# Both heads at once in the RWKV-7 core: products on four quarter tiles, joined evictions, and three reordered stage edges

## The reference

```python
def step(state, inp):
    r_t, w_t, k_t, v_t, a_t, b_t = inp
    sa = jnp.einsum('bhvk,bhk->bhv', state, a_t)
    state = state * w_t[:, :, None, :] + sa[..., None] * b_t[:, :, None, :] + v_t[..., None] * k_t[:, :, None, :]
    y = jnp.einsum('bhvk,bhk->bhv', state, r_t)
    return state, y
...
y = wkv7_scan(rf, decay, kd, vf, -kk, kk * a, reverse=(dirn == 1))
```

```python
q = rope_slice(rms_norm(q, q_gain), cos, sin, 0)
k = rope_slice(rms_norm(k, k_gain), cos, sin, 0)
```

## Time and profile before

| what | us |
|---|---|
| median of three runs | 2857.4 |
| lowest and highest run | 2849.94, 2857.96 |
| the profiled execution | 2856.87 |
| its span, first to last instruction | 2855.0 |
| PE busy | 2743.1 (96%) |
| DVE busy | 1465.4 (51%) |
| ACT busy | 1268.8 (44%) |
| POOL busy | 1127.8 (40%) |
| matmuls of the core's products, L779, busy | 291.5 |

### The profile page before, as it was taken

The page is one execution under the profiler, slowest core; times in us unless marked ns, Lnnn a source line. Parts: engine busy times, 40 slices in busy tenths (PEclk is TensorE's granted clock), DMA queues, the critical chain, the costliest instruction groups (busy, mean ns, idle before and its releaser), DMA issues.

```text
span 2855.0 us, 54997 instructions
## 1 busy us (share of the span) xinstructions
PE 2743.1 (96%) x23332; PEld 2187.8 (77%) x23332; DVE 1465.4 (51%) x2561; ACT 1268.8 (44%) x2296; POOL 1127.8 (40%) x634
## 2 busy tenths in 40 slices
PE   7899999979999999999999999999999999999999
PEld 5568888857778888877888876577777777788887
DVE  7865886057757777753888303612222224344410
ACT  5664443233556555644444225534444454422221
POOL 4124444534543332314444454034333443544443
PEclk9999999999999999999999999999999999999999
DMA  5102332322300000012233232023221332333232
GB/s 164 49 31 90 95 96 90 95 96 82 102 23 6 7 8 7 6 46 71 92 96 94 88 99 66 23 89 98 75 75 52 96 96 74 96 96 96 88 95 77
DMA packets 63460, 208.88 MB, mean 73 GB/s; under 512 B 11248, under 2 KB 11504, under 8 KB 62832
## 3 DMA queue, kind: packets, MB, share of 16 engines
q1 hardware_dynamic: 60704, 193.10, 21.9%
q0 software_dynamic: 1936, 10.91, 1.1%
q10 hardware_dynamic: 576, 1.35, 0.1%
HBM read 199.95 MB, written 4.19 MB: 72 GB/s over the span
## 4 chain that ended last, share of the span: by engine, by line
PE 86%; DVE 9%; ACT 2%; issue 2%; POOL 1%; DMA 0%; SPq 0%; DVEq 0%; ACTq 0%
PE banks L1658 21%; PE banks L1660 21%; PE banks L1659 21%; PE banks L779 9%; PE banks L1800 1%; DVE low L539 1%; PE banks L830 1%; DVE arena L2641 1%; PE banks L772 1%; PE banks L856 1%; PE banks L1776 1%; PE banks L1695 1%; PE banks L861 1%; PE banks L872 1%; PE banks L1848 1%
## 5 line engine op out<-in xcount | busy, mean ns | idle before, releaser
L312 POOL TENSOR_TENSOR low<-arena,high 128x1024 fp32r<-128x1024 f32 (+1 forms) x376 | 876.7, 2332 | 1328.8 <-ACT high L303 1328.7
L1658 PE MATMUL banks<-high,high 128*128 128x512 f32 (+1 forms) x2752 | 1093.4, 397 | 40.9 <-POOL low L312 24.1
L1660 PE MATMUL banks<-high,low 128*128 128x512 f32 (+1 forms) x2752 | 1082.3, 393 | 0.0
L1659 PE MATMUL banks<-low,high 128*128 128x512 f32 (+1 forms) x2752 | 1082.3, 393 | 0.0
L303 ACT ACTIVATE high<-arena 128x1024 fp32r<-128x1024 f32 (+1 forms) x376 | 381.9, 1016 | 800.9 <-PE banks L1660 799.5
L1658 PEld LDWEIGHTS banks<-high,high 128*128 128x128 f32 x2752 | 519.9, 189 | 171.6 <-POOL low L312 18.0
L1660 PEld LDWEIGHTS banks<-high,low 128*128 128x128 f32 x2752 | 519.9, 189 | 120.7
L1659 PEld LDWEIGHTS banks<-low,high 128*128 128x128 f32 x2752 | 520.2, 189 | 118.6 <-issue 1.9
L779 PE MATMUL banks<-arena 64*64 64x64 f32 x7680 | 291.5, 222 | 9.7 <-DVE arena L1544 3.4
L779 PEld LDWEIGHTS banks<-arena 64*64 64x64 f32 x7680 | 251.2, 135 | 58.1 <-issue 23.8
L2538 DVE TENSOR_TENSOR arena<-banks,arena 128x512 f32<-128x512 f32 x48 | 33.1, 691 | 425.1 <-PE banks L1660 423.9
(11 more groups left out here) (292 smaller groups left out, 2915.9 us busy)
## 6 DMA issues: line engine op xcount, KB each, us to landing
arena<-weights SPq DMA_DIRECT2D x302, 512.0 KB, 3.5
arena<-weights SPq DMA_DIRECT2D x48, 448.0 KB, 3.2
arena<-weights SPq DMA_DIRECT2D x28, 256.0 KB, 2.6
arena<-tables POOLq DMA_DIRECT2D x5, 448.0 KB, 3.6
arena<-x_t SPq DMA_DIRECT2D x4, 512.0 KB, 5.8
x_spill<-arena POOLq DMA_DIRECT2D x1, 2048.0 KB, 9.3
arena<-small_weights POOLq DMA_DIRECT2D x16, 128.0 KB, 2.6
arena<-x_spill POOLq DMA_DIRECT2D x1, 2048.0 KB, 9.3
```

The lines of the kernel that those rows point to most:

```text
L312: pool.tensor_tensor(lo[:, 0:n], ring[w % RING][:, 0:n], hi[:, 0:n].bitcast(F32), ALU.subtract).then_inc(w_low, 1)
L1658: pe.matmul(dst, hi[:, c], x[0], start=kt == 0, stop=False)
L1659: pe.matmul(dst, hi[:, c], x[1], start=False, stop=False)
L1660: mm = pe.matmul(dst, lo[:, c], x[0], start=False, stop=kt == kts_of[t] - 1)
```

## The change

Products. `both_heads` issues the products of both heads in one loop. Head 0 writes output half p from input half p as before, head 1 writes output half 1-p, each to the bank of its head, so the two fill all four quarters. S1, S2, U2, U5, U6, Q1 and Q2 go through it; S3, U3, U4 and T stay with `product`. Where head 1's result is the right factor of a later product, it lies in the other half of the partitions; for U2 POOL therefore writes U1 of head 1 a second time in swapped halves (UX, two instructions of 64x128 between U1_0 and U1_1).

Evictions. ACT copies S1, S2, Q1 and Q2 of both heads in one instruction of 128x512 over two banks, where it had two of 128x256; DVE adds U2, U5 and U6 in one of 128x256, where it had two of 128x128. Each waits for the second head's product, and the next product of either head waits for it. S1 waits for D_1 instead of D_0 for its first head.

Iteration 0. The table load goes ahead of S1's eviction, the copy of a1's hidden rows behind T's; POOL's k_sum goes ahead of the three low parts; the split of rw_g1's first tile goes to iteration 4.

Edges. (a) `sines(last)` goes behind `value(1)`, into the attention at its fourth step. (b) a_q's weights are split ahead of the biases, and each bias product follows one a_k tile. (c) Three score products go ahead of the last head sum, the fourth stays behind.

```diff
@@ def pe_rwkv
+        def both_heads(into, col, lhs, rhs):
+            last = [None, None]
+            for q in range(2):
+                for p in range(2):
+                    for h in range(2):
+                        last[h] = pe.matmul(into[h][hf(p ^ h), col + C * q:col + C * q + C], lhs(hf(p), h, q), rhs(hf(p), h, q),
+                                            start=True, stop=True)
+            return last
...
-        def square(i, h, s):
+        def square(i, s):
             if s == 1:
-                d2.wait(pe, i, f"D_{h}")
-                m, mt = (lambda r, q: R.D[r, h, q, :]), half_of(R.NM, h, 0)
+                d2.wait(pe, i, "D_1")
+                m, mt = (lambda r, h, q: R.D[r, h, q, :]), halves_of(R.NM, 0)
             else:
-                a2.wait(pe, i, f"S{s - 1}_{h}")
...
+                a2.wait(pe, i, "S1")
+                m, mt = halves_of(R.P2, 0), halves_of(R.P2, 1)
+            both_heads(PJ, 0, mt, m)
+            mm = both_heads(PJ, P, m, mt)
+            for h in range(2):
+                p2.inc(mm[h], f"S{s}_{h}")
...
+        def first_grow(i):
+            d2.wait(pe, i, "M_1")
+            g2.wait(pe, i, "U1_1")
+            mm = both_heads(PI, 0, halves_of(R.P2, 1), lambda r, h, q: R.UX[r, q, :] if h else R.U[i % 2][r, 0, q, :])
+            for h in range(2):
+                p2.inc(mm[h], f"U2_{h}")
...
+        def late_grow(i, m):
+            a2.wait(pe, i, f"Q{m}")
+            mm = both_heads(PI, 0, halves_of(R.P2, 1), halves_of(R.P2, 0))
...
+            d2.wait(pe, i, "U4_1" if m == 1 else "U5")
+            both_heads(PJ, 0, halves_of(R.NM, m), u)
+            mm = both_heads(PJ, P, u, lambda r, h, q: eye[r, :])
...
@@ the loop over iterations on PE
-                for s in (2, 3):
-                    for h in range(2):
-                        square(i, h, s)
-                        grow(i, h, s)
+                square(i, 2)
+                first_grow(i)
+                for h in range(2):
+                    last_square(i, h)
+                    grow(i, h, 3)
...
-                for h in range(2):
-                    merge(i, h, 1)
-                for h in range(2):
-                    grow(i, h, 5)
+                merge(i, 1)
+                late_grow(i, 1)
...
@@ def act_rwkv
+            def both(name, dst):
+                p2.wait(act, i, f"{name}_1")
+                a2.inc(act.activation(dst.rearrange("p h k b -> p h (k b)"), both_j[:, :, 0:256], ACT.Copy), name)
...
+                if i == 0:
+                    act.preload_act_table_set("natural_log_exp_and_others")
...
-                for h in range(2):
-                    ev("S1", h, flat(R.P2[:, h, :, :]), 256)
+                both("S1", R.P2)
...
@@ def pool_rwkv
                 d2.wait(pool, i, f"D_{h}")
+                if h:
+                    g2.wait(pool, i, "U1_0")
+                    for p in range(2):
+                        u_ = pool.tensor_tensor(R.UX[hf(1 - p), :, :], R.D[hf(p), 1, :, :],
+                                                eye[hf(p), :].unsqueeze(1).to_broadcast([C, 2, C]), ALU.add)
+                    g2.inc(u_, "UX")
+                    g2.wait(pool, i, "UX")
...
@@ def dve_rwkv
+            def add_both(s):
+                p2.wait(dve, i, f"U{s}_1")
+                u = R.U[i % 2].rearrange("p h q c -> p h (q c)")
+                d2.inc(dve.tensor_tensor(u, both_i[:, :, 0:P], u, ALU.add), f"U{s}")
...
@@ PE, before the memory attention
+            if seq[-1][0] == "c_q":
+                fill("c", 0, 3)
             small(len(seq))
             if seq[-1][0] == "c_q":
-                fill("c", 0, 4)
+                fill("c", 3, 4)
...
@@ POOL, before the differential attention
-        for h in range(4):
+        advance("a_q")
+        for h, t in enumerate(tiles_of["a_k"]):
+            advance_tiles([t])
             pool.tensor_scalar(B.biasA[:, h, :], B.dist, -SLOPE_A[h], None, ALU.mult).then_inc(bias_ready, 1)
-        advance("a_q", "a_k", "a_v")
+        advance("a_v")
...
@@ DVE, before and in the sliding-window attention
             sines(last - 1)
-            sines(last)
             value(1)
+            return lambda: sines(last)
...
             for s in range(len(PAIRS) + 7):
+                if s == 3:
+                    last_sines()
```

More of the change, by code:

```diff
@@ L825, in tokens, with merge @@
+        def merge(i, m):
+            u = lambda r, h, q: R.U[i % 2][r, h, q, :]
+            if m == 1:
+                a2.wait(pe, i, "T_1")
+            d2.wait(pe, i, "U4_1" if m == 1 else "U5")
+            both_heads(PJ, 0, halves_of(R.NM, m), u)
+            mm = both_heads(PJ, P, u, lambda r, h, q: eye[r, :])
+            for h in range(2):
+                p2.inc(mm[h], f"Q{m}_{h}")
         def tokens(i, h):
@@ L955, in pe_rwkv @@
             if off:
[L956 to L959 removed]
+                merge(i, 2)
+                late_grow(i, 2)
                 aux_left(i, 1)
@@ L1136, in act_rwkv @@
             if off:
-                for h in range(2):
-                    ev("S2", h, flat(R.P4[:, h, :, :]), 256)
-                if i == 0:
-                    act.preload_act_table_set("natural_log_exp_and_others")
-                    act.activation(R.h_high[1], R.a1h, ACT.Copy).then_inc(h_high, 1)
+                both("S2", R.P4)
                 if c == 3 and more:
@@ L1166, in act_rwkv @@
                     factor(j + 1, "F")
-                for h in range(2):
-                    ev("Q1", h, flat(R.P2[:, h, :, :]), 256)
+                both("Q1", R.P2)
                 if c == 0 and more:
@@ L1175, in act_rwkv @@
             if off:
-                for h in range(2):
-                    ev("Q2", h, flat(R.P2[:, h, :, :]), 256)
+                both("Q2", R.P2)
                 if c == 2 and j:
```

78 lines of the change are left out of this document (31 added, 47 removed).

## The result

The changed kernel takes 2862.09 us as the median of 16 runs (2859.41 to 2868.56); the kernel before, run 16 times in the same comparison, 2851.49 (2847.15 to 2857.96). The ratio is 1.0040, 95% interval 1.0032 to 1.0048: slower, by about 11 us. In this text PE "stands" where it is idle for a result of another engine; an "opening" is such a stand behind products whose eviction was joined. The 2857.4 on which the forecast stood was the median of three runs, and 6 us above that of the sixteen; the profiled execution of before was a high one as well. The time after lies above the range all the same, and on the other side of before than was forecast.

The account below looks back on a forecast made before the run. Core taken as bound by 64x64 products occupying the array, evictions nearly hidden. Core -5.0, edges -2.8 and -4.7 sum to -12.5 us from 2857.4: 2845 us; own range 2838 to 2853, full range 2832 to 2860.

Parts of the forecast that it names:

- S1 to U3 ... Gain 0: Core, each iteration from S1 to U3: 3.8 us before and 3.8 after, two joined evictions included, so no gain.
- Just hidden: price 0: POOL's U1_0, UX, U1_1 end 1.8 us after S1's start, U2 starts at 1.9: no cost, at most 6 us.
- So 0.3 of the 2.64 is left: Core, per iteration: four quarters save 2.64 us of array time, of which 0.3 remains after waits for joined evictions.
- -3+13 = +10: Core's joined products: -3 us forecast; four openings, each 0.1 us longer or shorter over 32 iterations, give 13 either way.
- 0.2 was given back for D_1: Core, per iteration: S1 waits for D_1, one DVE instruction later (0.28 us), partly covered by auxiliary products: 0.2 us lost.
- rival 5: Clock falls for PE's stands in the core: sixteen 6.8 us half-clock stretches lose 3.4 each, +54 us, 2899; chance 0.03.
- The first iteration: Core's iteration 0: reordering removes PE stands of 1.35 and 2.58 us; -3.5 us taken, ends -4 and -1.5.
- Edges (a) and (b): First attention's 5.50 us stand before the values, -2.8 us; a_q's weight split with 3.01 us stand and half clock, -4.7.
- Edge (c): Three score products ahead of a head sum where PE stands 2.07 us; later products released as before: 0.
- 1: Rival: two banks cost as two instructions, +21.6 us on evictions and +5 on U5's sums, 2872; chance 0.06.
- 2: Rival: the shared PSUM bank keeps the pace at 30 ns, nothing saved, waits remain, +84 us, 2929; chance 0.04.
- Rival 3: Gains are eaten, attention keeps DVE's pace: -3 us for the edges, 0 for the core, 2854; chance 0.22.

Follow-up runs that it names:

- run 16: Not a run's label but a count, in "run 16 times": the unchanged kernel before was measured 16 times, median 2851.49 us.
- The filler: The changed kernel with 32 records of unread products behind Q1 and again behind Q2: 2857.15 us, ratio 1.0021 to the kernel before.
- the kernel with nothing joined: The kernel before with the three stage edges and the change's order of iteration 0, no product, eviction or sum joined: 2837.95 us, ratio 0.9948.
- the core alone: The changed kernel without the three stage edges, only the RWKV-7 core changed: 2874.72 us, ratio 1.0076 to the kernel before.
- the edges alone: The kernel before with the three stage edges and no other piece of the change: 2844.36 us, ratio 0.9968.

## Why the prediction was wrong, step by step

- **What bounds the core; the price of each new instruction.** Right for the most part: 15 ns a record, 597 ns for two banks and 0.42 for 128x256 stood as taken. PE hands over to ACT in 0.09, not 0.05, so an opening is 0.74 and not 0.7. POOL's second U1 takes 0.79 with c = 1, 2 and 3 (0.45 with c = 0), not 0.46; why isn't shown.
- **"S1 to U3 ... Gain 0", with "Just hidden: price 0" for POOL's UX, in the sum "So 0.3 of the 2.64 is left", -3 us.** This step failed. Measured in undisturbed periods the core's change is +0.30 us an iteration, +9.4 over 31, near the upper end that the text had, -3+13 = +10. The parts are read from the starts of the same products in single undisturbed iterations of both traces (c = 0, 1, 2, 3):
  - S1 to U3 is 0.07, 0.08, 0.45 and 0.39 longer, 0.25 on the mean where 0 was taken. Two openings, each 0.04 longer than worked out, come to the 0.07. The rest is POOL's chain: U1_0, UX and U1_1 end 2.5 us after D_0, not 2.0, PE stands 0.26 for it before U2 and then up to 0.34 for the sum of U2. Without PE's wait for U1_1, 0.17 of the 0.30 went.
  - S1 starts 0.24 later on the mean (0, 0.20, 0.41, 0.34), where 0.2 was given back for D_1, though with c = 1 it is the sum of U6 that PE waits for, and the 29 waits on which that 0.2 stood are 10 of products and 19 of weight loads.
  - Q1 and U5 gain 0.14, not 0.25: with c = 3 nothing is gained, since the solve waits 0.31 for X.
  - Q2 and U6 gain 0.03, not 0.05: they lose 0.14 with c = 0 and 1 and gain 0.2 with c = 2 and 3.

  The forecast took the openings one by one; the periods add the next wait behind each.
- **The clock.** Nothing in the sum, and 0.03 as rival 5, only as one that falls often. It did in part: 41 us at half clock in the core, where rival 5 had 109. What I took as evidence against it, 12 us with 5.1 of stand at full clock, was one place. The filler shows 6 to 7 us of cost, 0.18 us for each of the 37.6 us that went with it, where rival 5 took 0.5; and the kernel with nothing joined, which has no openings, has no such stretch.
- **The first iteration.** Forecast -3.5. In the changed kernel its period is 14.7 against 17.9, -3.2, with a half-clock stretch at its end; in the core alone and with the filler, without that stretch, 14.02, -3.9; with nothing joined 13.32, -4.6. Of the two terms beside it, +0.8 for the split in iteration 4 measured 0 (14.54 with nothing joined, as with the edges alone), and +0.7 for the last iteration 0.1 (from its start to rw_o 23.89 against 23.75).
- **Edges (a) and (b).** Forecast -2.8 and -4.7. (b) measured -4.5. (a) brought PE's start 4.5 us forward and 6.0 are left at the end of the attention: the sines were hidden there, their price of 1.5 was not paid, and one half-clock stretch (at 110 us) did not come back.
- **Edge (c).** Forecast 0, measured 0, but the text ahead misread it: `fill` issues slices of the next big tile's products (mix2's), not scores. Nine of them now cover the 2.07 us, and PE then stands 1.64 before the scores for the same chain.
- **The rivals.** 1 and 2 fell: two banks cost one instruction, and the pace was reached. Rival 3 named what happened, another engine close behind, but gave it 0 for the core and 2854.
- **The base.** The three runs of before on which the forecast stood had a median 6 us above that of sixteen.

The change as a whole is slower because joining the heads costs more than the rest gives. The edges and the order of iteration 0 alone come to 0.9948 of before, with the joining it is 1.0040: 26 us. In the traces the 31 periods of the core are 488.5 against 463.9. Of these 24.5 us, roughly, 6.6 went with the filler. Of the 17.9 that it left, 0.7 are the first period (14.02 against 13.32), 4.7 the last three (49.4 against 44.7), and 8.2 are 27 periods at the undisturbed rate of 0.30 (61.88 against 60.66 for four). The other 4.3 lie scattered, about half of them in the first eight periods; what makes these and the last three long wasn't tried. Nor was the array's gain without the joined evictions: no run has four quarters with each head evicted by itself.

## What to carry to other kernels

Two streams that cover each other's evictions are a resource: making the array faster by merging them moves its time into waits, and what counts is the period, measured with everything in it, not PE's busy time (here the busy time of four iterations fell by 14% and they took 2% longer). Where the forecast is a small difference of two large terms, the sign belongs to the waits that come second, such as the helper engine's chain that was "just hidden". When a loop is given openings, look also at what the clock does with them, and change the pieces of such a bundle one at a time: its parts here had opposite signs.

## What the runs showed of the hardware

- The clock went to half behind stretches in which PE was busy for 84 to 85% and never stood longer than 0.75 us; products that nobody reads, put into the openings, brought it back (mean of the core 0.96 to 1.00) and the time down by 5 us.
- ACT's copy of 128x512 out of two banks took 597 ns, the same as out of one.
- 64x64 products of both input halves, written into different halves of the partitions of one bank, ran at 15 ns a record: 32 in 0.69 us, against 1.20 on two quarters.
- On POOL, 64 partitions by 128 elements took 451 ns, as long as 128 by 128 did before (460 on the mean): half the partitions saved nothing.
- The runs of the core alone spread over 19 us, those of the kernel with nothing joined over 1.7. Openings alone don't explain that: the sixteen of the changed kernel spread over 9, the sixteen of before over 11.
